# VectorE's order within a step: the recurrence ahead of the weights' low parts and the tile's sum

## The reference, cut to what matters

```python
def first_block(x, c, w_ada, ...):
    mod = silu(c) @ w_ada + b_ada                  # 6 vectors of 2048: 12288 x 2048 weights
    sh1, sc1, gt1, sh2, sc2, gt2 = split(mod, 6)
    h = rmsnorm(x) * (1 + sc1) + sh1
    p = h @ w_in
    y_rwkv = rwkv7_mixer(p[:, :rwkv_columns], ...) # below
    y_pool = pool_mixer(p[:, rwkv_columns:], ...)
    x = x + gt1 * (concat(y_rwkv, y_pool) @ w_out)
    h = rmsnorm(x) * (1 + sc2) + sh2
    return x + gt2 * conv_ffn(h, ...)

# rwkv7_mixer: p = p + mu * (shift(p) - p); r, k, v and decay, rates, gate from p; kk = k * k_k over its norm
def step(S, r, w, k, v, a, b):                     # for each token and head; a = -kk, b = kk * rate
    S = S * w + (S @ a)[:, None] * b + v[:, None] * k
    return S, S @ r
# then a norm of y per head, a bonus (r k r_k) v is added, and the gate multiplies
```

## Time and profile before

| | us |
|---|---|
| median of 3 runs | 2822.28 (2815.01 to 2830.18) |
| the profiled execution's own time | 2819.87 |
| its span, first to last instruction | 2818.1 |
| TensorE busy (matmuls) | 2697.9 |
| VectorE busy | 1825.9 |
| ScalarE busy | 1260.3 |
| mean granted clock of TensorE | 0.979 |

### The profile page before, as it was taken

How to read it: one execution, slowest core, us unless ns; L and a number is a source line. 1 busy time by engine, 2 the same in 40 slices (tenths; PEclk the granted TensorE clock), 3 DMA queues, 4 the chain that set the end, 5 groups by cost and what they waited for, 6 DMA issues and landing times.

```text
span 2818.1 us, 47810 instructions
## 1 busy us (share of the span) xinstructions
PE 2697.9 (96%) x17516; PEld 2224.6 (79%) x17516; DVE 1825.9 (65%) x2529; ACT 1260.3 (45%) x1712; POOL 143.7 (5%) x149
## 2 busy tenths in 40 slices
PE   5799999989999999999999999999999999999998
PEld 0357667777888888888888888887878888888887
DVE  0455565666877777755576676678577777776554
ACT  1432222244555555544443355643455555554443
POOL 1001100321000000010100000000100000000000
PEclk7799999999999999999999999999999999999999
DMA  9776655434555555555555544444545555555553
GB/s 401 286 293 252 236 229 227 173 115 162 187 193 188 184 193 192 185 205 208 196 185 180 192 163 153 162 164 166 192 161 182 189 183 187 185 183 205 206 197 134
DMA packets 82701, 554.73 MB, mean 197 GB/s; under 512 B 8496, under 2 KB 8624, under 8 KB 17840
## 3 DMA queue, kind: packets, MB, share of 16 engines
q1 hardware_dynamic: 81888, 550.21, 53.1%
q10 hardware_dynamic: 720, 3.21, 0.3%
HBM read 551.29 MB, written 2.10 MB: 196 GB/s over the span
## 4 chain that ended last, share of the span: by engine, by line
PE 86%; DVE 6%; DMA 3%; ACT 2%; issue 2%; DVEq 0%; SPq 0%; ACTq 0%
PE bank L516 52%; PE bank L517 26%; DMA raw<-in_stream_dram 3%; PE bank L559 2%; DVE wlo L1460 1%; PE bank L683 1%; DVE yb L1476 1%; PE bank L697 1%; PE bank L693 1%; DVE zmat L1695 0%; DVE t L1583 0%; DVE yb L2065 0%; PE bank L775 0%; PE bank L781 0%; PE bank L768 0%
## 5 line engine op out<-in xcount | busy, mean ns | idle before, releaser
L516 PE MATMUL bank<-act,whi 128*128 128x512 f32 x4976 | 1785.2, 403 | 24.4 <-DVE act L1497 20.9
L517 PE MATMUL bank<-act,wlo 128*128 128x256 f32 x4976 | 1396.5, 281 | 0.0
L516 PEld LDWEIGHTS bank<-act,whi 128*128 128x128 f32 x4976 | 940.7, 189 | 279.3 <-issue 38.6
L1460 DVE TENSOR_TENSOR wlo<-raw,whi 128x1024 fp32r<-128x1024 f32 x846 | 1035.2, 1232 | 177.8 <-ACT whi L1034 171.5
L1034 ACT ACTIVATE whi<-raw 128x1024 fp32r<-128x1024 f32 x846 | 883.5, 1052 | 438.4 <-PE bank L517 409.0
L517 PEld LDWEIGHTS bank<-act,wlo 128*128 128x128 f32 x4976 | 944.8, 190 | 3.6 <-issue 3.4
L516 PE MATMUL bank<-ff,whi 128*128 128x512 f32 x1408 | 493.2, 393 | 1.0 <-DVE wlo L1460 1.0
L517 PE MATMUL bank<-ff,wlo 128*128 128x256 f32 x1408 | 392.8, 279 | 0.0
L516 PEld LDWEIGHTS bank<-ff,whi 128*128 128x128 f32 x1408 | 263.8, 187 | 64.6 <-DVE wlo L1460 1.6
L517 PEld LDWEIGHTS bank<-ff,wlo 128*128 128x128 f32 x1408 | 263.8, 187 | 0.0
L1476 DVE TENSOR_REDUCE joined<-bank 128x256 f32<-128x512 f32 x179 | 123.4, 691 | 212.2 <-PE bank L517 212.0
(11 more groups left out here) (236 smaller groups left out, 1518.4 us busy)
## 6 DMA issues: line engine op xcount, KB each, us to landing
raw<-in_stream_dram SPq DMA_DIRECT2D x519, 1024.0 KB, 4.8
x<-in_x_dram SPq DMA_DIRECT2D x1, 2048.0 KB, 14.4
lora_w<-in_lora_dram SPq DMA_DIRECT2D x1, 1536.0 KB, 11.6
pool_w<-in_pool_w_dram ACTq DMA_DIRECT2D x1, 1024.0 KB, 8.8
out_dram<-x SPq DMA_DIRECT2D x2, 512.0 KB, 2.8
out_dram<-x ACTq DMA_DIRECT2D x2, 512.0 KB, 3.0
catt<-in_att_dram ACTq DMA_DIRECT2D x1, 576.0 KB, 3.4
par<-in_params_dram SPq DMA_DIRECT2D x1, 541.5 KB, 3.3
```

Of the source, the lines that this page charges most:

```text
L516: nc.tensor.matmul(tile_bank(t), wh, flat(pair[:, kt]), start=starts and n == 0, stop=False)
L517: mm = nc.tensor.matmul(small_half(t), wl, pair[:, kt, 0], start=False, stop=stops and last)
L1460: nc.vector.tensor_tensor(wlo[:, k % RING], raw[:, r % RING, 8 * (k % 2):8 * (k % 2) + 8], whi[:, k % RING].bitcast(F32), ALU.subtract).th ...
```

## The change

In segments 1 to 4, VectorE runs the recurrence's operations of a step at the step's start, for steps 0 to 12. The low part and the sum of the tile come after them. In steps 13 and 14 the order stays as it was. The token shift and the preparation stay behind all three. No other engine's program changes.

```diff
             def segment(s):
                 last = s == SEGMENTS - 1
                 for n in range(17):
+                    if s and n < 13:
+                        recurrence(n, s - 1)
                     h = half_started(s, n) if n < 16 else None
                     if h is not None:
                         cut_lo(2 * FIRST_CHUNK["wkv"] + wkv_half(s, h) + 2)
...
-                    if s:
+                    if s and n >= 13:
                         recurrence(n, s - 1)
                     if m is not None:
                         shifted_tile(s, m)
```

## The result

The changed kernel takes 2883.4 us (2877.7 to 2899.4, 4 runs) against 2818.7 us; the ratio is 1.0246, 95% interval 1.0211 to 1.0282. It is slower by some 69 us by the ratio, which is made from all repeated runs and so isn't exactly that of the medians (they are 64.8 apart); differences in us behind a ratio are worked out from it in all that follows. The forecast was +52 on the profiled execution, in a range from 2848 to 2893. The profiled execution took 2882.6 us with a span of 2880.9, 62.8 more than before.

What follows compares the result with a forecast made beforehand. TensorE, busy for 96% of the span, was taken as the bound, any new stop paid in full. 3 x (13.4 dead time + 4.2 clock) - 0.5 = 52.3 us on 2819.9 gave 2872; own range 2860 to 2888, wider 2848 to 2893.

Steps and rivals of the forecast that it cites:

- Step 1: Low part behind the `zmat` copy delays the second modulation chunk of step 2: new TensorE wait of 2.1 us a segment.
- Step 7: Low part behind `u_out` and `s_out` delays three transfers; TensorE waits 4.8 us a segment for two chunks.
- The chain of steps 8 and 9: Late sum of step 8's tile delays ScalarE's `wide`, which TensorE's output step needs: 3.1 us a segment.
- Steps 10 and 11: Sum of step 10's tile follows `s_out`, so `wide` comes after TensorE wants it: 2.1 us a segment.
- Steps 4 and 12: Late low parts delay transfers, about 6 us in step 4, 2.9 in step 12; both covered, counted as nothing.
- Dead time: Sum of TensorE's new waits in segments 1 to 3: 13.4 us a segment; segment 4 counted separately at -0.5.
- The clock: TensorE's granted clock goes low after new stops of steps 2, 8 and 9: 4.2 us a segment, bounds 0 to 8.6.
- Rival (e): Clock stays at its lower level from step 7 to step 11 as stops follow closely: +74 us, 2896; chance 0.10.
- (a): Faster: VectorE answers earlier, TensorE's waits for it and the low-clock stretches behind `us` go: -15 us, 2807; chance 0.04.
- (b): No change: late low parts are covered everywhere, small gains at four places: -4 us, 2818; chance 0.04.
- (c): Only the chain through ScalarE to `wide` costs, 5.8 us a segment plus about 1.4 clock: +21, 2843; chance 0.10.
- (d): Only late transfers cost, ScalarE's tiles in time: 8.2 us a segment plus 2.2 clock: +31, 2853; chance 0.10.

Runs made afterwards that it cites:

- step 1 alone: Kernel before, with the recurrence ahead of the low part only in step 1 of segments 1 to 3: 2836.3 us, ratio 1.0052.
- step 7 alone: Kernel before, with the recurrence ahead of the low part only in step 7 of segments 1 to 3: 2848.3 us, ratio 1.0089.
- step 12 alone: Kernel before, with the recurrence ahead of the low part only in step 12 of segments 1 to 3: ratio 0.9995.
- only the low part late: Kernel before, with only the low part moved behind the recurrence, the sum staying ahead, steps 0 to 12, segments 1 to 4: 2876.2 us, ratio 1.0199.
- only the sum late: Kernel before, with only the tile's sum moved behind the recurrence, the low part staying first, steps 0 to 12, segments 1 to 4: 2840.5 us, ratio 1.0080.
- second halves first: Whole change, but steps 1, 4, 7, 9, 12 of segments 1 to 3 keep the old order, so ring slots return in time: 2846.2 us, ratio 1.0102.
- three moves: Kernel before, segments 1 to 3: step 15's low part cut in step 13, key-norm reciprocal split around `r_out`, `ar` products behind `y_out`: 2791.2 us, ratio 0.9892.

## Why the prediction was right, point by point

**What bounds it** held: VectorE's own time in the windows is 58 to 62 us a segment in all kernels, and what was lost shows as TensorE's waits (37.7 us) or as its slower work (27.7 us). The windows grow to 118 to 123 us, and TensorE nowhere waits for a low part itself between 212 and 640 us.

**Step 1** (2.1 us): waits of 2.0, 5.0 and 2.6 us in the three segments. In segment 2 the lone price of 4.7 us was wrong. Three more transfers were issued within 3.3 us behind it, and it landed after 7.6. In the kernel with step 1 alone late these waits are 2.0, 2.5 and 2.5 us.

**Step 7** (4.8 us): 5.6, 5.8 and 4.3 us in the profile after, both chunks taken together; with step 7 alone late 5.8, 4.1 and 3.8.

**The chain of steps 8 and 9** (3.1 us): 1.8, 1.6 and 1.7. In the prediction TensorE came on time; in fact it came later, as its work behind the chunks of step 8 ran at the lower clock. With the ring in time it is up to 3.3. **Steps 10 and 11**: 2.3 us in all three against 2.1 forecast; the chunk of step 10 is waited for 4.7, 3.2 and 3.0 us in place of the old 2.2 for `us`.

**Steps 4 and 12** cost nothing, as said: 0.5 us once in step 6, and step 12 alone 0.9995.

**Dead time** as a sum: 3 x 13.4 - 0.5 = 39.7 forecast, 37.7 measured. That it is so close is in part luck: over three segments steps 1 and 7 came out 4.5 us above the forecast and the chain of steps 8 and 9 4.2 below. Steps 6, 10 and 11 add 1.6, and from step 14 to the start of the next segment 4.4 us came back where 0.5 was counted.

**The clock is the term that was mis-sized**: 4.2 us a segment forecast, 27.7 / 3 = 9.2 measured, above even my upper bound of 8.6. Not its price per us but its amount was wrong. I had taken some 10 us a segment more at the lower level and at most 20.5; it was 25, with single stretches of 17.1 us in segments 2 and 3 behind the stops of step 8. Rival (e), with a chance of 0.10, had about this amount, with too high a price, and the 65.4 us of the windows lie between its 74 and the forecast's 52. The measured 2883.4 us is near the upper end, 2888, of the forecast's own range: what the clock took beyond its bound, the dead time and the rest of the program gave back. Its reason, that each stop follows close on the other, isn't shown: the kernel with only the low part late has the same 17.1 us with waits of only 0.8 us in them. What sets how long the clock stays low is open. The price, (change of the windows - change of the waits) / change of the low time, comes out alike in kernels of both signs. Here the low time is added up from the single low stretches of each trace:

| kernel | windows | waits | low time | us per low us |
|---|---|---|---|---|
| whole change | +65.4 | +37.7 | +75.1 | 0.37 |
| only the sum late | +23.8 | +13.2 | +27.3 | 0.39 |
| only the low part late | +56.2 | +26.8 | +64.9 | 0.45 |
| step 7 alone | +27.4 | +10.8 | +44.4 | 0.37 |
| step 1 alone | +13.3 | +7.7 | +17.1 | 0.33 |
| second halves first | +20.0 | +12.5 | +20.5 | 0.37 |
| three moves | -25.5 | -15.0 | -27.3 | 0.38 |

It is 0.42 in the prediction. The Trainium skill ("TensorE: Matmul & The Clock Gate", the terms at its start) would give 0.5; the measurement decides. Part of the difference is low time in which TensorE waits, and where the clock costs nothing: it was busy in 82.7 of the 102.4 low us after and in 24.0 of the 27.3 before, and half of the 58.7 us between them is 29.4, near the 27.7 measured. It isn't all, since the same sum gives 0.48 for step 1 alone and 0.42 for step 7 alone, where 0.33 and 0.37 were measured.

**The rivals.** (a) and (b), the faster and the unchanged case, fell by the ratio. (c) and (d) each hold for a part, but neither is the whole: the chain alone is +23 us, near (c)'s 21, and the ring alone +56, well above (d)'s 31, with 26.8 us of waits and 64.9 us more low time. What stays open is why transfers issued together land up to 3 us apart from case to case. No run here varied that.

## What to carry to other kernels

Before an instruction is moved behind others, ask what its end releases besides its result: here a ring slot and through it a transfer that was wanted 7 us later. An engine with 35% idle time is no proof of slack, since what counts is the order around the few signals that open a gate. Put the signals that open a gate first, fill the waits with work that nobody waits for, and count a stop of TensorE at about twice its length where its clock falls behind it (1.6 to 2.5 times in the kernels of the table). Only the first of the three moves was run alone, so what the other two are worth singly isn't shown.

## What was not expected of the hardware

After a stop of 2.2 us the granted clock went low for 3.41 us in one segment and for 6.83 in the next, with the same work around it; behind the stops of step 8 in the changed kernel for 17.1, and for as long in the kernel with only the low part late, where TensorE was busy for 16.3 of them. And matmuls by zero weights, put in to fill the stops, took 10.4 us out of the three windows of the changed kernel although they add some 25 us of work to TensorE (whole kernel 2883.4 and 2873.3 us, with overlapping intervals).
